# Piece counts, sample steps and two TensorE waits in the mLSTM chain of a hybrid decoder step

## The reference

```python
m_i = jnp.maximum(jnp.max(dlog, axis=3), inter)
s = jnp.einsum('bcihd,bcjhd->bcijh', qc, kc) * jnp.exp(dlog - m_i[:, :, :, None, :])
num = (jnp.einsum('bcijh,bcjhv->bcihv', s, vc)
       + sc[..., None] * jnp.einsum('bcihd,bchdv->bcihv', qc, c_b))
hid = num / jnp.maximum(jnp.abs(den), jnp.exp(-m_i))[..., None]
o_ml = jax.nn.sigmoid(om) * (_rmsnorm_heads(hm).reshape(bsz, t_len, ML_W) * lp['ml_norm'])
mix = jnp.concatenate([o_rw, o_ret, o_ml], -1).astype(x.dtype) @ lp['w_out']
```

## Time and profile before

| | |
|---|---|
| median of 3 runs | 2771.86 us (2770.22 to 2775.87) |
| the profiled execution | 2775.89 us, of which the span of the trace is 2774.1 us |
| TensorE matmuls busy | 2691.8 us (97%) |
| VectorE busy | 1625.7 us (59%) |
| ScalarE busy | 1163.1 us (42%) |
| DMA mean share of 16 engines | about 54%, 161 GB/s |
| mean granted TensorE clock | 0.989 of full speed |

### The profile page before, as it was taken

The page is one execution under the profiler, slowest core; times in us unless marked ns, Lnnn a source line. Parts: engine busy times, 40 slices in busy tenths (PEclk is TensorE's granted clock), DMA queues, the critical chain, the costliest instruction groups (busy, mean ns, idle before and its releaser), DMA issues.

```text
span 2774.1 us, 55696 instructions
## 1 busy us (share of the span) xinstructions
PE 2691.8 (97%) x23575; PEld 2632.0 (95%) x23575; DVE 1625.7 (59%) x1770; ACT 1163.1 (42%) x1460; POOL 0.2 (0%) x4
## 2 busy tenths in 40 slices
PE   7999999999999999999999999998999999999997
PEld 7988899899999999999999998988999999999997
DVE  5566547678454545545586574577875554545444
ACT  4445334446333333333354453343553333333332
POOL 0000000000000000000000000000000000000000
PEclk9999999999999999999999999999999999999999
DMA  7544325365666666556564542253666666665653
GB/s 231 170 130 114 97 85 163 113 170 178 181 181 182 179 178 181 177 180 182 178 203 140 173 124 77 85 162 93 192 190 181 178 179 181 181 182 177 212 176 115
DMA packets 280391, 447.43 MB, mean 161 GB/s; under 512 B 45175, under 2 KB 76337, under 8 KB 279929
## 3 DMA queue, kind: packets, MB, share of 16 engines
q1 hardware_dynamic: 278600, 441.59, 53.6%
q10 hardware_dynamic: 1618, 3.31, 0.4%
HBM read 433.06 MB, written 11.78 MB: 160 GB/s over the span
## 4 chain that ended last, share of the span: by engine, by line
PE 89%; DVE 7%; ACT 2%; issue 2%; ACTq 0%; DMA 0%; DVEq 0%; SPq 0%
PE psum L693 19%; PE psum L694 19%; PE psum L695 19%; PE psum L724 6%; PE psum L726 6%; PE psum L725 6%; DVE w_lo L1750 2%; ACT w_hi L1318 1%; PE psum L714 1%; PE psum L921 1%; PE psum L715 1%; PE psum L716 1%; PE psum L1092 1%; PE psum L1077 1%; PE psum L1081 1%
## 5 line engine op out<-in xcount | busy, mean ns | idle before, releaser
L1746 DVE TENSOR_TENSOR w_lo<-w_raw,w_hi 128x1024 fp32r<-128x1024 f32 x496 | 606.1, 1225 | 683.1 <-ACT w_hi L1305 682.0
L1305 ACT ACTIVATE w_hi<-w_raw 128x1024 fp32r<-128x1024 f32 x504 | 533.7, 1060 | 890.0 <-PE psum L695 867.3
L693 PE MATMUL psum<-x_hi,w_lo 128*128 128x264 f32 (+3 forms) x3072 | 877.8, 286 | 2.1 <-DVE x_lo L2073 1.0
L694 PE MATMUL psum<-x_lo,w_hi 128*128 128x264 f32 (+3 forms) x3072 | 874.9, 285 | 0.0
L695 PE MATMUL psum<-x_hi,w_hi 128*128 128x264 f32 (+3 forms) x3072 | 874.5, 285 | 0.0
L693 PEld LDWEIGHTS psum<-x_hi,w_lo 128*128 128x128 f32 x3072 | 579.5, 189 | 3.4 <-issue 1.3
L694 PEld LDWEIGHTS psum<-x_lo,w_hi 128*128 128x128 f32 x3072 | 580.8, 189 | 0.2
L695 PEld LDWEIGHTS psum<-x_hi,w_hi 128*128 128x128 f32 x3072 | 579.6, 189 | 0.0
L1750 DVE TENSOR_TENSOR w_lo<-w_raw,w_hi 128x1024 fp32r<-128x1024 f32 x304 | 368.4, 1223 | 208.4 <-ACT w_hi L1318 192.0
L1318 ACT ACTIVATE w_hi<-w_raw 128x1024 fp32r<-128x1024 f32 x292 | 304.4, 1055 | 294.3 <-PE psum L726 210.7
L724 PE MATMUL psum<-x_hi,w_lo 128*128 128x264 f32 (+1 forms) x1376 | 412.7, 300 | 5.3 <-ACT p_tail L1341 2.1
(11 more groups left out here) (502 smaller groups left out, 2530.9 us busy)
## 6 DMA issues: line engine op xcount, KB each, us to landing
w_raw<-in_w_in SPq DMA_DIRECT2D x192, 512.0 KB, 3.7
w_raw<-in_w_gate SPq DMA_DIRECT2D x176, 512.0 KB, 3.7
w_raw<-in_w_up SPq DMA_DIRECT2D x176, 512.0 KB, 4.1
w_raw<-in_w_down SPq DMA_DIRECT2D x176, 512.0 KB, 3.7
w_raw<-in_w_out SPq DMA_DIRECT2D x64, 512.0 KB, 4.0
w_raw<-in_w_in SPq DMA_DIRECT2D x16, 262.0 KB, 2.9
r_sample<-in_state_ret SPq DMA_DIRECT2D x6, 512.0 KB, 7.3
out_s_ret<-r_sample SPq DMA_DIRECT2D x6, 512.0 KB, 5.5
```

The lines of the kernel that those rows point to most:

```text
L693: mm(out, w1, bh[:, k, 0:nt], start=(k == 0), stop=False)
L694: mm(out, w0, bl[:, k, 0:nt], start=False, stop=False)
L1305: A(wh[:, j, :, :], raw[:, j, :, :], ACT.Copy).then_inc(S.hi_ready, 1)
L1746: TT(wl[:, j, :, :], raw[:, j, :, :], wh[:, j, :, :].bitcast(F32), ALU.subtract).then_inc(S.lo_ready, 1)
```

## The change

1. Piece counts. The positions of the steps move: turn0 from tile 40 to 44, turn1 45 to 49, score 50 to 54, num0 59 to 63, num1 stays at 70, vt 76 to 74, v0 stays at 90, and all later ones stay.
2. VectorE scales the sample state before the copies of num0 (pairs 0 and 1) and of num1 (pair 2), not after num1 (pair 0) and after the sample streams (pairs 1 and 2). Its wait for the load of the sample state moves with it.
3. ScalarE squares the sample columns of `a_y` before its background parts of step sumsq, not after.
4. VectorE multiplies the last two heads (line 2040) at once after the first four, runs one background part, makes both `o_lo`, and only then runs the other background parts of spread1. ScalarE likewise rounds the last two heads after one background part.
5. TensorE no longer waits for `a_done` ahead of line 1208 (it waits ahead of the first `kblock`), and the wait for all 4 banks of the last group is split: bank n waits only for its own copy.

```diff
-    ml_steps = [('spread_m', 14), ('spread_e', 12), ('turn0', 14), ('turn1', 5), ('score', 5), ('num0', 9), ('num1', 11),
-                ('vt', 6), ('v0', 14), ('v1', 5), ('v2', 5), ('sy', 7), ('syt', 5), ('sumsq', 10), ('spread', 16), ('spread1', 6)]
+    ml_steps = [('spread_m', 14), ('spread_e', 12), ('turn0', 18), ('turn1', 5), ('score', 5), ('num0', 9), ('num1', 7),
+                ('vt', 4), ('v0', 16), ('v1', 5), ('v2', 5), ('sy', 7), ('syt', 5), ('sumsq', 10), ('spread', 16), ('spread1', 6)]
...
                 for n in range(blocks):
+                    if free is not None:
+                        pe.wait_ge(S.bank_free, free + n + 1)
...
                 attention(l, True, 2 * l + 1, bg)
-                pe.wait_ge(S.a_done, 3 * l + 2)
                 tr(ps[0:AP_ * NS + AP_, 7, 0:128], mnf[:, :], ident).then_inc(S.state_turned, 1)
...
                     if g == 0:
-                        pe.wait_ge(S.bank_free, freed(l, IN_GROUPS + 3))
+                        pe.wait_ge(S.a_done, 3 * l + 2)
...
-                        kblock(s + i // 2, i % 2, 10 + i, 4 * (g % 2), oh, ol, 10, KB - 1)
+                        kblock(s + i // 2, i % 2, 10 + i, 4 * (g % 2), oh, ol, 10, KB - 1,
+                               free=freed(l, IN_GROUPS + 2) if g + i == 0 else None)
...
-                bg.to('sumsq')
+                if not ml:
+                    bg.to('sumsq')
                 act.wait_ge(S.a_y_ready, n + 1)
                 if ml:
                     A(sq[:, :, SEQ:T], ay[:, :, SEQ:T], ACT.Square).then_inc(S.a_squares, 1)
+                    bg.to('sumsq')
...
                     A(oh[:, 10:14, :], ay[:, 0:4, :], ACT.Copy).then_inc(S.a_out_hi, 1)
-                    bg.to('spread1')
+                    bg.step()
                     act.wait_ge(S.a_out, n + 1)
                     A(oh[:, 14:16, :], ay[:, 4:6, :], ACT.Copy).then_inc(S.a_out_hi, 1)
+                    bg.to('spread1')
...
                     bg.to(f'num{c}')
+                    if ml:
+                        dve.wait_ge(S.a_sample_loaded, 48 * (n + 1))
+                        for p in ((0, 1), (2,))[c]:
+                            own(TT(sam[:, p, :, :], sam[:, p, :, :], over(msk[:, p, :], 128), ALU.mult))
                     dve.wait_ge(S.a_summed, 2 * n + c + 1)
...
-                dve.wait_ge(S.a_sample_loaded, 48 * (n + 1))
-                if ml:
-                    own(TT(sam[:, 0, :, :], sam[:, 0, :, :], over(msk[:, 0, :], 128), ALU.mult))
...
-                if ml:
-                    for p in range(1, AP_):
-                        own(TT(sam[:, p, :, :], sam[:, p, :, :], over(msk[:, p, :], 128), ALU.mult))
+                    dve.wait_ge(S.a_sample_loaded, 48 * (n + 1))
...
-                bg.to('spread1')
+                if not ml:
+                    bg.to('spread1')
                 dve.wait_ge(S.a_spread, 2 * n + 2)
                 if ml:
                     TT(ay[:, 4:6, :], ay[:, 4:6, :], ps[:, 4:6, 0:T], ALU.mult).then_inc(S.a_out, 1)
+                    bg.step()
                     for i, hs in enumerate((slice(0, 4), slice(4, 6))):
...
+                    bg.to('spread1')
```

More of the change, by code:

```diff
@@ L704, in groups, with kblock @@
                                 kblocks - 1, bh, bl, nt, ready=ready if j < slabs else None)
-            def kblock(s, half, k, bank0, bh, bl, first, last_k, blocks=4, nt=T):
+            def kblock(s, half, k, bank0, bh, bl, first, last_k, blocks=4, nt=T, free=None):
                 if not half:
```

## The result

The changed kernel takes **2754.45 us** (median of 4 runs, 2752.72 to 2756.43), the kernel before beside it 2771.50. The medians differ by 17.05 us. The ratio of the two, taken over all their runs, is 0.9934, with a 95% interval of 0.9922 to 0.9946: 18 us faster, 15 to 22 by the interval. The forecast was 2753.3 us, 18.6 less than before.

What follows compares the result with a forecast made beforehand. TensorE carries 89% of the chain, so its waits and half-speed clock bound the time. Idle falls 6.87 us a layer, twice 13.7, plus 4.9 of clock: 18.6 off the 2771.86 median gives 2753.3 us, range 2748 to 2764.

Steps and rivals of the forecast that it cites:

- Both waits on copies: TensorE's waits on a group's copies out, 2.66 us at turn0 and 0.45 at tile 81, would both go.
- The new wait at num0: TensorE would wait 1.02 us on `a_scores`, as VectorE makes slab 9's low part before weighting the scores; bounds 0 and 2.66.
- two figures for the table switch: ScalarE's table load before the sigmoid: 1.28 us by the trace, or 1.38 more of drain by the Trainium skill page.
- -1.68: At v1, moving the sample scaling earlier on VectorE would remove TensorE's whole 1.68 us wait on the sample state.
- the 0.17 forecast: The 0.83 us wait at sumsq would go, leaving a new 0.17 wait at spread: net -0.66 a layer.
- The late thing: At the tail, slab 20's low part would be late: 1.72 us on `w_lo` replaces 1.93 and 2.23, net -2.44.
- the signs named ahead: In TensorE's waits: lines 1660, 1998, 1451 gone, `a_scores` near 1.0, `w_lo` near 1.7; clock 1.00 after both tails' starts.
- The sum: Idle per layer from 9.78 to 2.91 us, -6.87; twice -13.7; clock -4.9; together -18.6 us.
- The three terms: Half-speed stretches won back: 2.1 us after the first layer's tail gap, 1.5 after the second's, 1.3 after turn0's gap.
- The rival that the clock falls all the same: Half speed still comes after the new gaps or elsewhere: 2758 us, range to 2761; chance 0.18.
- gain was given back: Rival: in the feed-forward, weights arrive at the DMA's pace, not TensorE's, so the gain is lost: 2771 us; chance 0.08.
- The slower rival: VectorE's moved wait for the sample load holds up num0's copy and num1: 2783 us if landing at 530; chance 0.04.

Runs made afterwards that it cites:

- n1: Changed kernel with VectorE weighting the scores before its background part of step score, not after; 2751.08 us, ratio 0.9924 to the kernel before.
- u1: Changed kernel with all the old piece counts put back; 2758.35 us, ratio 0.9943 to the kernel before.
- u2: Changed kernel with the sample scaling back behind num1 and the sample streams; 2758.88 us, ratio 0.9946 to the kernel before.
- u3: Changed kernel with the sample squares back behind the background parts of sumsq; 2753.57 us, ratio 0.9924 to the kernel before.
- n2: Changed kernel with the third pair of residual operations on VectorE moved from part 16 to 19, behind slabs 20 to 22; 2745.52 us, ratio 0.9909.
- u5: Changed kernel with both old TensorE waits back (`a_done` ahead of line 1208, all four banks) but the new order; 2751.30 us, ratio 0.9923.
- u6: Changed kernel with the whole old tail: old order of the last heads and both old TensorE waits; 2757.79 us, ratio 0.9946.
- n4: Changed kernel with scores weighted before the background part, the third residual pair moved later, and both old TensorE waits back; 2745.95 us, ratio 0.9906.
- l1: Changed kernel with the three sample-state loads issued beside output-projection slabs 11 to 13, not 4 to 6; 2760.20 us, ratio 0.9951.
- u4: Changed kernel with the old order of the last heads on ScalarE and VectorE, keeping the new TensorE waits; 2759.09 us, ratio 0.9940.

## Why the prediction was right

**Part 1.** Both waits on copies went, as worked out. The new wait at num0 came at the place and on the engine foretold, 0.82 for 1.02: TensorE reached num0 5.1 us after it had started score, and not the 4.9 taken from before. The weights ended 5.87 us after score's start, for 5.89 forecast. n1 shows that the step was right. Of the two figures for the table switch that the prediction sets side by side the lower one held, since a longer switch would have made this wait longer and not shorter: after the change the load starts at 505.73, takes 1.28, and the sigmoid starts at 507.02. u1 prices the part at 2.5 us a layer without the clock.

**Part 2.** -1.68 was the wait in the kernel before, and the chain confirms that it is gone. u2 adds what the sum missed: taken by itself, among the other parts, it is worth 2.76.

**Part 3.** 0.83 gone and 0.26 left for the 0.17 forecast; u3 confirms both halves.

**Parts 4 and 5.** The late thing was the low part of slab 20, 1.85 for 1.72. n2 shows it, against the name in the view of waits. That the split is worth nothing here is shown by u5 (0.05), and u6 and n4 show where it would be (0.74 and 0.62). Of the signs named ahead one was off by its name only: the wait at the tail does not stand under `w_lo`.

**The sum.** Idle time per layer went from 9.78 to 0.82 + 0.26 + 1.85 = 2.93, 6.85 less for the 6.87 forecast. The chain shrank by more, 91.80 - 84.13 = 7.67. The term mis-sized is the wait itself: it costs more than its recorded idle time. Between u2 and after, 2.37 us of idle are 2.76 of chain; between n1 and after, 0.79 less idle are 1.09 of chain. So a wait had 0.2 to 0.4 us on top here, which I had set at zero: three waits fewer made 0.8 a layer. The rows show where most of it lies. A matmul's row is 0.28 us long, but without a wait the next starts 0.12 after it; the recorded idle begins only at the row's end. Ahead of num0 the last matmul starts at 511.00 and num0 at 512.10: 1.10 apart, 0.98 more than without the wait, for 0.82 of recorded idle. Num0's own row is then 0.10 longer than in n1 (1.60 for 1.50), and 0.98 + 0.10 is the 1.09 of the chain.

**The clock.** The three terms were 2.1, 1.5 and 1.3. The second does not come out of its rows: worked out as the first was, give 3.50 - 19 x 0.122 = 1.2, not 1.5. The tails show 1.57, so the higher figure was the better one, but no row of the prediction gave it. In the two profiled executions the three stretches gave back 2.19 + 1.57 + 1.29 = 5.05 us for 4.9 (tails 37.23 and 36.61 to 35.04, and the second chain's excess). The sum for the changed stretches is 7.67 + 8.95 + 2.19 + 1.57 = 20.4, and the spans differ by 19.7.

The medians differ by 17.05 only. That the median came within 1.2 us of the forecast is therefore in part luck: the chains gave 1.6 us more than forecast, and the medians lie 2.7 less apart than the spans. One reason is on record. The kernel before was profiled in one of its slower executions, at a mean clock of 0.989; of its 27 timed runs beside the experiments those at 0.989 took 2774.5 to 2776.3 us and those at 0.991 2769.7 to 2771.4. The 4.9 us of clock were read from that one execution and taken off the median whole. The rival that the clock falls all the same may be another part: behind the same gap of 1.85 to 1.92 us the tail ran 1.54 longer in 4 of 14 cases (once in u3, once in n1, twice in l1). Those four are in other kernels; in the changed kernel's own trace the clock fell behind neither gap. The rest may be scatter in stretches that the change does not touch: the identical work ahead of the first chain took from 481.51 to 487.14 us. How the 2.7 us divide is argued and not shown, since each kernel has one trace, and a timed run has only its mean clock on record.

**The others.** No gain was given back: what follows the last tail took 796.58 us before and 796.89 after. The slower rival had its mechanism (l1) and not its condition.

## What to carry to other kernels

Where engines interleave by counts, a moved count also moves what stands ahead in the other engines' queues: work out each goal, and see what is then ahead of the instruction that someone waits for. Ask of each wait that goes what is late next, and of a gap named "issue" or named after an unlikely operation what ended 0.1 us before it. A wait on TensorE costs somewhat more than its recorded idle: take the distance between the starts. When edits are worth 1 to 3 us in a time that scatters by 5, compare the length of the stretch between two landmarks in the traces, which here agreed between the layers to 0.02 us where the clock held.

## What the runs showed of the hardware

The scatter of the times is in the granted clock. The same instructions ahead of the first chain, in after and in u2_scaling (columns: length, PE busy and matmuls, clock, DMA share, GB/s):

```profile
0.00:487.14 487.14, 453.15 (x4416) 0.98 0.48 142
```

```profile
0.00:481.51 481.51, 448.53 (x4415) 0.99 0.48 143
```

The same work takes 5.6 us less with a clock 0.01 higher. The clock records of all 14 traces say the same: the stretch ahead of the first chain took 481.5 to 482.3 us where 13.7 us of it were granted half speed (3 traces), 483.8 to 484.0 with 17.1 us (4), and 485.1 to 487.1 with 20.5 us (7). Between the first tail and the second chain it took 1227.3 to 1228.0 with 3.4 us at half speed, and 1232.0 to 1232.4 with 13.7. Behind the last tail no trace shows half speed until the last 15 us of the span, and there all 14 took 796.5 to 797.0.

Of the gaps ahead of a tail, none cost the clock at 0 or 0.37 us (0 of 8) and some at 1.85 to 1.92 (4 of 14). All did at 3.6 in one piece (u4) or at 4.1 to 4.2 in two with the turn of 0.29 us between (before, u6): 6 of 6. The price was 1.54 us wherever the gap was under 4; behind the double gaps it was 1.57 to 2.34. Inside the chain the gap of 2.66 (before, u1) cost the clock in 2 of 4 cases. My sum had taken gaps under 2 us as free, with a chance of 0.18 against it.
